# Projecting the first three chunks from tokens modulated by scale alone, with shift added afterwards

## The reference

```python
cond = jax.nn.silu(c)
mod = cond @ w_ada + b_ada                       # (1, 6 * 1024)
sh1, sc1, gt1, sh2, sc2, gt2 = jnp.split(mod, 6, axis=-1)
h = rms_norm(x, g_pre_mix) * (1.0 + sc1) + sh1
zin = h @ w_in                                   # 24 chunks of 128 columns
cv_val, cv_gate, q, f, i, og = jnp.split(zin, splits, axis=-1)
out_a = conformer_conv(cv_val, cv_gate, ...)     # sigmoid gate, 31 taps, layer norm, silu
out_b = hgrn2(q, f, i, og, ...)
mix = jnp.concatenate([out_a, out_b], axis=-1) @ w_out
x = x + gt1 * rms_norm(mix, g_post_mix)
# then the gated feed-forward part, with sh2, sc2, gt2
```

## Time and profile before

| | us |
|---|---|
| median of 3 runs | 1127.62 |
| lowest and highest | 1127.52, 1127.94 |
| span of the profiled execution, first to last instruction | 1124.7 |
| PE busy in it | 1089.5 (97%) |
| DVE busy in it | 823.3 (73%) |

### The profile page before, as it was taken

The page is one execution under the profiler, slowest core; times in us unless marked ns, Lnnn a source line. Parts: engine busy times, 40 slices in busy tenths (PEclk is TensorE's granted clock), DMA queues, the critical chain, the costliest instruction groups (busy, mean ns, idle before and its releaser), DMA issues.

```text
span 1124.7 us, 14554 instructions
## 1 busy us (share of the span) xinstructions
PE 1089.5 (97%) x5140; PEld 907.7 (81%) x5140; DVE 823.3 (73%) x1168; ACT 498.9 (44%) x815; POOL 751.2 (67%) x645
## 2 busy tenths in 40 slices
PE   2899999999999999999999999999999999999996
PEld 1688888888888888888888888888888888888885
DVE  5977997979998755678775767666666666666658
ACT  5665575574652834345333323333333333233334
POOL 4179666675773640427977777868686969696966
PEclk9999999999999999999999999999999999999999
DMA  9644332333311271202322222222221222222217
GB/s 330 198 143 136 99 111 74 115 94 95 94 38 38 70 249 75 93 26 80 92 68 65 76 66 71 71 63 71 62 77 58 74 68 66 70 63 74 66 48 297
DMA packets 104745, 107.49 MB, mean 96 GB/s; under 512 B 6525, under 2 KB 84578, under 8 KB 104674
## 3 DMA queue, kind: packets, MB, share of 16 engines
q1 hardware_dynamic: 103216, 102.26, 29.0%
q10 hardware_dynamic: 1458, 4.31, 1.0%
HBM read 98.16 MB, written 8.40 MB: 95 GB/s over the span
## 4 chain that ended last, share of the span: by engine, by line
PE 94%; DVE 2%; ACT 1%; SPq 1%; issue 1%; DMA 1%; DVEq 0%; ACTq 0%
PE pair L2235 34%; PE pair L2041 23%; PE pair L2255 17%; PE pair L2144 8%; PE pair L2077 2%; PE pair L2198 2%; PE pair L2278 2%; PE pair L2004 1%; DMA x<-in_x 1%; DVE acc L1403 1%; PE pair L2072 1%; PE pair L2091 1%; PE pair L1965 1%; SPq L541 1%; PE pair L2093 1%
## 5 line engine op out<-in xcount | busy, mean ns | idle before, releaser
L1826 DVE TENSOR_TENSOR yt<-yt,pair 128x512 f32<-128x512 f32 x264 | 176.2, 684 | 34.6 <-PE pair L2255 34.6
L1524 DVE SCALAR_TENSOR_TENSOR pair<-u,conv_w_col,pair 128x512 f32<-128x512 f32 x208 | 139.6, 750 | 1.9 <-ACT pair L1120 1.4
L844 POOL TENSOR_TENSOR raw_r<-raw,w_hi 128x512 fp32r<-128x512 f32 x68 | 96.3, 1417 | 65.1 <-ACT w_hi L1256 65.1
L756 POOL TENSOR_TENSOR acc<-acc,ada 128x256 f32<-128x256 f32 x112 | 92.1, 854 | 55.9 <-ACT ada L1057 54.6
L2255 PE MATMUL pair<-w_hi,op_hi 128*128 128x512 f32 x280 | 109.2, 390 | 0.0
L2255 PE MATMUL pair<-w_hi,op_lo 128*128 128x512 f32 x280 | 109.0, 389 | 0.0
L2255 PE MATMUL pair<-w_lo,op_hi 128*128 128x512 f32 x280 | 108.9, 389 | 0.0
L853 POOL TENSOR_TENSOR w_lo<-w_lo_f,w_hi 128x512 fp32r<-128x512 f32 x70 | 95.1, 1359 | 0.0
L2235 PE MATMUL pair<-t_lo,w_hi 128*128 128x512 f32 x240 | 93.7, 390 | 0.0
L2235 PE MATMUL pair<-t_hi,w_hi 128*128 128x512 f32 x240 | 93.4, 389 | 0.0
L744 POOL TENSOR_TENSOR w_lo<-raw,w_hi 128x256 fp32r<-128x256 f32 x84 | 66.9, 828 | 23.1 <-ACT w_hi L1013 22.9
(11 more groups left out here) (330 smaller groups left out, 2951.0 us busy)
## 6 DMA issues: line engine op xcount, KB each, us to landing
ada<-in_w_ada SPq DMA_DIRECT2D x48, 512.0 KB, 3.9
raw<-in_w_ffn_in SPq DMA_DIRECT2D x56, 256.0 KB, 3.0
raw<-in_w_in SPq DMA_DIRECT2D x24, 512.0 KB, 3.8
w_lo_f<-in_w_ffn_out SPq DMA_DIRECT2D x40, 256.0 KB, 3.1
w_hi_f<-in_w_ffn_out SPq DMA_DIRECT2D x30, 256.0 KB, 3.1
x<-in_x SPq DMA_DIRECT2D x8, 512.0 KB, 8.2
raw<-in_w_out SPq DMA_DIRECT2D x8, 512.0 KB, 3.4
x<-in_x SPq DMA_DIRECT2D x4, 1024.0 KB, 8.7
```

Source lines behind the costliest of these rows:

```text
L756: i_ = pool.tensor_tensor(acc[:, cols], acc[:, cols], ada[:, n % 2, cols], ALU.add)
L844: pool.tensor_tensor(place_part(at), place_full(at), place_part(GU_HIGH[m % 3]), ALU.subtract).then_inc(gu_low, 1)
L1524: i_ = dve.scalar_tensor_tensor(out=dst, in0=tap_of(j + 1, h), scalar=tap_weight(j + 1, t), in1=dst, op0=ALU.mult, op1=ALU.add)
L1826: i_ = dve.tensor_tensor(dst, dst, bank(4 + t), ALU.add)
```

## The change

Chunks 0, 1 and 2 (gate, val and i of the first head) are projected from tokens that carry scale only. The part of shift is put in later: as a bias for these three chunks, one number per output column, that PE makes from the unsplit weights (`first_biases`, 24 products with one column), and for all later chunks by writing the high and low token parts anew with shift added (`shifted_high` on ACT, `shifted_low` on DVE). So:

- Ada's scale and shift columns are loaded and summed apart: four blocks of 256 scale columns, the second of them ahead of x's second half, and two halves of 512 shift columns after them. Four rows of the second shift half are multiplied by ACT and added by POOL.
- The three first chunks have their own raw tiles (`first_raw`), and are loaded and split in halves on POOL; the late masks are made before these splits.
- Chunk 2 goes into `pair[3]`, with the turning of the shift sums (`shift_sums`) and the biases placed between its parts.
- `full_and_high` writes into `x0` itself, `u` is made with the biases (`gated_first`), and `TAPS_FIRST` is smaller for the first two heads.

```diff
-            load_block(0)
+            load_scales(0)
             for i in range(TT):
                 if i == 4:
-                    for g in range(RAW):
-                        load_chunk(g)
+                    load_first(0, 0)
+                    load_first(1, 0)
+                    load_scales(1)
                 sp.dma_start(x0[:, i, :], x_d[:, i, :]).then_inc(x_loaded[i], 16)
-            for b in range(1, 4):
-                load_block(b)
-            for g in range(RAW, 5):
-                load_chunk(g)
-            sp.wait_ge(h_ready, 16)
+            load_first(0, 1)
+            load_first(1, 1)
+            load_scales(2)
+            load_scales(3)
+            load_first(2, 0)
+            load_first(2, 1)
+            load_shifts(0)
+            sp.wait_ge(acc_ready, 2)
+            load_shifts(1)
+            load_chunk(WS)
+            load_chunk(WS + 1)
+            sp.wait_ge(bias_ready, 1)
...
+            def split_first(g, q):
+                cols = slice(q * HALF, (q + 1) * HALF)
+                pool.wait_ge(first_loaded_w[2 * g + q], 16)
+                me.done(pool.tensor_copy(w_hi[:, g, cols], first_raw[g][:, cols]))
+                me.wait()
+                pool.tensor_tensor(w_lo[:, g, cols], first_raw[g][:, cols], w_hi[:, g, cols], ALU.subtract
+                                   ).then_inc(w_split if q else first_split, 1)
...
             mask_late()
-            pool.wait_ge(h_ready, 16)
-            me.wait()
+            for q in range(2):
+                for g in range(2):
+                    split_first(g, q)
+            pool.wait_ge(ss_ready, TT)
+            for q in range(2):
+                split_first(2, q)
+            add_late_shifts()
+            low(WS)
+            pool.wait_ge(again_ready, KT)
             pool.memset(pmat[:, :, :], 0.0).then_inc(p_clear, 1)
...
+            def shifted_high(kt):
+                act.wait_ge(shift_ready, kt // 4 + 1)
+                if kt < KT - 1:
+                    act.wait_ge(first_used, kt + 1)
+                else:
+                    act.wait_ge(w_used, WS)
+                dst = (ha_hi if kt < 4 else hb_hi)[:, kt % 4, :]
+                act.activation(turns_of(dst), x0[:, :, kt * P:(kt + 1) * P], ACT.Identity, bias=mod[:, kt:kt + 1]
+                               ).then_inc(again_hi, 1)
...
+            def gated_first():
+                dve.wait_ge(*chunk_freed(0))
+                dve.wait_ge(w_used, 2)
+                val, by = pair[1], first_bias[:, 1:2]
+                dve.scalar_tensor_tensor(out=u[:, TAPS - 1:TAPS - 1 + HALF], in0=val[:, 0:HALF], scalar=by, in1=sg[:, 0:HALF],
+                                         op0=ALU.add, op1=ALU.mult)
...
+            def first_biases():
+                pe.wait_ge(shift_ready, 2)
+                for g in range(WS):
+                    for kt in range(KT):
+                        i_ = pe.matmul(bank(4)[:, 4 + g:5 + g], first_raw[g][:, kt * P:(kt + 1) * P], mod[:, kt:kt + 1],
+                                       start=kt == 0, stop=kt == KT - 1)
+                i_.then_inc(bias_made, 1)
...
+            def project_first():
+                pe.wait_ge(w_split, WS)
+                for kt in range(KT):
+                    hi, lo = (ha_hi, ha_lo) if kt < 4 else (hb_hi, hb_lo)
+                    split_product(pair[3], 2, slice(kt * P, (kt + 1) * P), hi[:, kt % 4, :], lo[:, kt % 4, :],
+                                  kt == 0, kt == KT - 1).then_inc(first_used if kt < KT - 1 else w_used, 1)
+                    if kt == 1:
+                        shift_sums(0)
+                    if kt == 3:
+                        shift_sums(1)
+                    if kt == 5:
+                        first_biases()
...
+                    if g == 2:
+                        if kt == 0:
+                            project_first()
+                        continue
...
+                    if g == WS:
+                        pe.wait_ge(again_ready, kt + 1)
```

More of the change, by code:

```diff
@@ L218, in build @@
         cond = keep("cond", [P, KT])
+        first_bias = keep("first_bias", [P, WS])
         gs = keep("gs", [P, 2, KT])
@@ L545, in load_chunk @@
             def load_chunk(g):
[L546 removed]
+                ready = g - 1 if g >= WS + RAW else None
                 if g < N_IN:
@@ L1150, in ln_step @@
                     act.preload_act_table_set("silu_and_others")
-            act.wait_ge(h_ready, 16)
+            high(WS)
+            for kt in range(KT - 2):
+                shifted_high(kt)
             evacuate(0)
-            high(WS)
+            for kt in range(KT - 2, KT):
+                shifted_high(kt)
+            act.wait_ge(vec_ready, 3)
             for period in range(5):
@@ new lines, in sum_late_shifts @@
+            def sum_late_shifts():
+                for j in range(KT // 2, KT):
+                    dst = acc_shift[:, 1, j % 2, :]
+                    if j == KT // 2:
+                        dve.wait_ge(shifts_loaded[3], 16)
+                    if j < KT // 2 + 2:
+                        me.done(dve.tensor_scalar(dst, shifts_late[:, j, :], cond[:, j:j + 1], None, ALU.mult))
+                    else:
+                        me.wait(behind=1)
+                        me.done(dve.scalar_tensor_tensor(out=dst, in0=shifts_late[:, j, :], scalar=cond[:, j:j + 1], in1=dst,
+                                                         op0=ALU.mult, op1=ALU.add))
+                me.wait()
+                me.done(dve.tensor_tensor(acc_shift[:, 1, 0, :], acc_shift[:, 1, 0, :], acc_shift[:, 1, 1, :], ALU.add))
+                me.wait()
+                dve.wait_ge(late_shift_added, KT // 2 - 1)
+                dve.tensor_tensor(acc_shift[:, 1, 0, :], acc_shift[:, 1, 0, :], shifts_late[:, 0, :], ALU.add
+                                  ).then_inc(late_shift_summed, 1)
@@ new lines, in scale, with shift @@
+            def scale(kt):
+                dve.wait_ge(mod0_summed, kt + 1)
+                dve.scalar_tensor_tensor(out=gs[:, 0, kt:kt + 1], in0=bank(4 + 2 * (kt % 2))[:, 0:1],
+                                         scalar=scale_bias[:, kt:kt + 1], in1=vec[:, ROW_GPRE1 + kt:ROW_GPRE1 + kt + 1],
+                                         op0=ALU.add, op1=ALU.mult).then_inc(mod0_ready, 1)
+            def shift(b):
+                cols = slice(4 * b, 4 * b + 4)
+                dve.wait_ge(shift_turned, b + 1)
+                dve.tensor_tensor(mod[:, cols], bank(4 + b)[:, 0:4], vec[:, ROW_BADA + 4 * b:ROW_BADA + 4 * b + 4], ALU.add
+                                  ).then_inc(shift_ready, 1)
@@ L1973, in mod_sums, with shift_sums @@
                     pe.wait_ge(full0_ready, 2 * kt - 3)
-                for s_ in range(2):
-                    first = s_ * 2 * P + kt % 2 * P
-                    i_ = pe.matmul(bank(4 + 2 * (kt % 2))[:, s_:s_ + 1], acc0[:, kt // 2 % 2, 0, first:first + P],
-                                   ones[:, 0:1], start=True, stop=True)
-                i_.then_inc(mod0_summed, 1)
+                pe.matmul(bank(4 + 2 * (kt % 2))[:, 0:1], acc_scale[:, kt // 2 % 2, 0, kt % 2 * P:(kt % 2 + 1) * P],
+                          ones[:, 0:1], start=True, stop=True).then_inc(mod0_summed, 1)
+            def shift_sums(b):
+                pe.wait_ge(*((late_shift_summed, 1) if b else (shift_summed, 1)))
+                pe.wait_ge(mod0_ready, KT)
+                column_sums(acc_shift[:, b, 0, :], bank(4 + b), 4).then_inc(shift_turned, 1)
+            def first_biases():
[5 more added lines that the diff above has]
+                i_.then_inc(bias_made, 1)
             def turn_x(g):
@@ L2018, in _ @@
             turn_x(3)
-            for g in range(3):
-                project_group(g)
+            project_group(0)
+            project_group(1)
             mod_sums(2)
             mod_sums(3)
+            turn_x(4)
+            project_group(2)
+            turn_x(5)
             project_group(3)
-            turn_x(4)
-            turn_x(5)
             turn_x(6)
-            for g in range(4, 16):
+            project_group(4)
+            turn_x(7)
+            project_group(5)
+            mod_sums(4)
+            mod_sums(5)
+            project_group(6)
+            turn_x(8)
+            turn_x(9)
+            project_group(7)
+            turn_x(10)
+            project_group(8)
+            turn_x(11)
+            project_group(9)
+            mod_sums(6)
+            mod_sums(7)
+            project_group(10)
+            turn_x(12)
+            turn_x(13)
+            project_group(11)
+            turn_x(14)
+            project_group(12)
+            turn_x(15)
+            for g in range(13, 16):
                 project_group(g)
-                if g % 2 == 0 and g // 2 + 2 < KT:
-                    mod_sums(g // 2 + 2)
-                if g + 3 < 16:
-                    turn_x(g + 3)
             def split_product(dst, slot, w_cols, x_hi, x_lo, first, last):
```

240 lines of the change are left out of this document (154 added, 86 removed).

## The result

The changed kernel takes 1143.81 us (median of 4 runs, 1142.22 to 1144.91), the kernel before 1127.57 beside it: ratio 1.0144, 95% interval 1.0130 to 1.0159. It is slower by 16.2 us. The forecast said slower, by 5.6, and its range ended at 1137.3. The profiled execution spans 1140.7 us, 16.0 more than before.

What follows compares the result with a forecast made beforehand. PE's own work was taken to bound the kernel, so a later start ends later one for one. Terms +1.5 - 3.8 + 7.6 + 0.4 gave +5.7, stated as 1133.2 us, range 1129.0 to 1137.3.

Steps and rivals of the forecast that it cites:

- own sign of being wrong: Forecast fails if chunk 3 starts before 79 us or PE waits over 3 us behind that start.
- T: End of VectorE's normalisation of the last tile: 27.7 us before, forecast 29.2, +1.5.
- T to A: From last tile's normalisation to last matmul of chunks 0 and 1: 37.3 us becomes 33.5, -3.8.
- 0.6 and 0.7 for groups 14 and 15: PE waits allowed in chunks 0 and 1, where ScalarE has four shift rows among groups 11 to 15.
- 0.4 for GpSimd's split: Allowance in chunks 0 and 1 for GpSimd splitting chunk 2 beside VectorE: 0.4 us.
- A to Z: From last matmul of chunks 0 and 1 to chunk 3's start: 11.7 us becomes 19.3, +7.6.
- the biases' 5.3: In chunk 2, 24 one-column products as 48 instructions at 0.11 us each: 5.3 us.
- rival 1: PE's clock falls in the biases' second half and next matmuls: +3 us, 1136; chance 0.14.
- Behind Z: From chunk 3's start on, work is kept; new waits from VectorE and GpSimd queues add 0.4 us.
- POOL 0 to 2 us late there: GpSimd's ada rows, started later against PE, reach slot M of the first head 0 to 2 us late.
- rival 2: Queues behind chunk 3's start late: GpSimd misses slot M by 3 us, VectorE's taps push slots; 1137; chance 0.08.
- no row here shows a drop: Argument about PE's clock falling in the biases: the profile rows show no drop behind one-column products.

Runs made afterwards that it cites:

- kernel with four edits: Changed kernel with ada additions before weight 7's low part, biases in three groups, all late rows on VectorE, chunks 0 and 1 biases copied early: 1133.93 us.
- kernel with three edits: Changed kernel with ada additions before weight 7's low part, biases in three groups, GpSimd's late shift additions behind the last low part: 1135.73 us.
- last kernel: Kernel with four edits, plus scale's second block behind x, GpSimd's splits held until its sums end, one late tap sum behind the ada additions: 1131.91 us.

## Why the prediction was wrong

The direction held, and so did the main mechanism: chunk 3 started later than before, since the shift work and the biases weigh more than the head gains. The time was 10.6 us too low, by the steps below. The prediction's own sign of being wrong, a wait of over 3 us behind chunk 3's start, came true.

- **T, +1.5: right** (+1.3). The loads landed as reckoned from the bytes, ScalarE on tile 4 at 19.14 for 19.0. A row of 256 columns took 0.42, I had 0.40. The contention with the splits was about 2 us: 0.8 in the last normalisation (1.56 for 0.75), 0.2 in the one before it, 0.6 in the small subtraction and 0.3 in the last addition.
- **T to A, -3.8: mis-sized, -1.9 measured.** I had allowed 0.6 and 0.7 for groups 14 and 15 and 0.4 for GpSimd's split. The step that failed is that GpSimd's three shift additions have no term in this sum: they are off PE's path, but stop VectorE, which is on it. Moved away, they gave 1.6 us back here. With ScalarE's four products gone too and VectorE summing all rows, T to A was 32.3, below the forecast. Another 0.7 came from the slow start: the first two groups took 4.85 for 4.15. That term was not to be forecast: from profile to profile of the changed kernels with this head it goes from 3.8 to 5.1. The Trainium skill, "SBUF — State Buffer", section "Who interferes with whom", says that such instructions of VectorE and GpSimd exclude each other for a whole instruction. The trace agrees, 1.77 and 1.75 for 0.74 and 0.69; I had weighed that rule at T and not here.
- **A to Z, +7.6: mis-sized, +9.7.** With the clock whole the kernel with four edits has 19.3 too, though otherwise made up: 5.6 us of biases, 0.5 of waiting for the late sum and none for `u`. The failed term is the biases' 5.3: they took 6.2 and left a low clock on the last two parts of chunk 2 (kt 6 and 7), which took 5.1 for 2.7. That is rival 1, near its price (2.4 plus 1.3 less 1.0, forecast; 0.9 plus 2.4 less the wait for `u`, measured, 2.1 over the forecast). Rival 1 let the clock fall in the middle of the row; here it fell in the last third and stayed low longer behind it. Where it falls differs too: in the profiles of five changed kernels the same row takes 5.3 to 7.3.
- **Behind Z, +0.4: wrong, +6.9.** "POOL 0 to 2 us late there" was the step. Its work behind Z was 6.6 us more than before (memset, a low part and an addition, 0.95 + 2.83 + 2.83, which used to lie ahead of Z), and it began 2.8 us after Z. That is 9.4. Against it stood 2.2 between its last addition and slot M and 5.1 idle behind Z (2.3, 1.3 and 1.5 us); I had counted 7 idle and only part of the work. That leaves 2.1. Another 0.9 is new idle time at 97.9, for ScalarE's product, and 0.4 is contention with VectorE, which hardly grew: the low part of weight 7 took 4.78 for 2.83, but the eight additions behind it 6.67, where they had taken 8.12 before. So it missed slot M by 3.37, as in rival 2. And I priced a wait as its own length, while PE's clock fell behind it: 3.4 became about 6.7.
- **The chances.** I gave rivals 1 and 2 0.14 and 0.08, as if they were separate and small. Rival 1's mechanism, a low clock behind little work, is what doubles rival 2's wait: in all five profiles with a wait of 2.5 us or more in slot M of the first head the 16 sums behind it took 2.97 to 3.55 instead of 1.84. And "no row here shows a drop" was true of the rows read, not of the trace: the kernel before has one at 332 us, behind the 0.7 that the earlier trace rows list. It would have made both rivals likelier.

The Trainium skill, "TensorE: Matmul & The Clock Gate", section "What's actually happening", says that the throttled clock is the default and activity releases it. The trace agrees: 48 instructions with one column leave 0.50, 16 products of 512 columns in the wait keep 1.00. I had the rule in rival 1 and looked for such a drop only in the first part of the trace.

One thing stays open. Behind waits of 1.7 to 2.5 us the clock sometimes fell and sometimes did not: in the kernel with three edits it stayed whole behind the same 1.74 us for the late sum, where it fell with one of them. And it fell behind the 16 sums of slot M in that same kernel with no wait ahead of them (0.68 from 128 to 132 us). The runs of one kernel differ in it, in the last kernel by about 3 us each time. Which of two equal executions gets it, no row shows.

## What to carry to other kernels

A wait of PE can cost more than its length when little stands around it: price it twice, once as given and once with the next few microseconds at half clock, and let no row of one-column products grow long; break it up between wide matmuls, which here made a low clock rarer and did not exclude it. Before calling such a fall of the clock unlikely, look for one in the whole trace of the kernel at hand. When a stage is pushed later, list for every helper engine what it used to finish ahead of the mark and now must do behind it; idle time counts only where it lies between that work and the deadline. And an addition given to an idle GpSimd is not free if VectorE works in SBUF beside it: the wait goes wherever the two meet.

## What the runs showed of the hardware

- 16 matmuls of 512 columns, run for nothing in a wait of PE, made the kernel 4.2 us faster (3.1 us at that place in the traces): the 16 column sums behind it took 1.84 instead of 3.30.
- The wait need not be long: behind 16 column sums and a wait of 0.7 us the granted clock fell in the profiles of 14 of the 16 kernels, the one before the change among them (0.57 from 332 to 336 us).
- 24 full-precision products of 128x128 by one column cost 4.3 us in three groups of 8 and 9.6 us in one row, in an otherwise unchanged kernel. PE counts as busy for all of the row, and the granted clock still falls to 0.50 in it.
- VectorE's work of 0.69 to 0.75 us in SBUF took 1.56 to 1.77 us beside GpSimd, for normalisations, multiply-adds and plain subtractions alike, whichever piece of work GpSimd had there (casts and splits of weights, additions of shift rows). With GpSimd's additions moved away the time came back at that place and went at the next.
